# Output projections as seven block products a pair of tiles

## The reference

```python
    y = ... @ w_out                              # output projection, 2048 x 2048
    x = _layernorm(DEEPNORM_ALPHA * x + y, post_ln_g[i], post_ln_b[i])
    x = x + (p[i] @ ple_w[i]) * jax.nn.sigmoid(x @ ple_gate_w[i])
```

## Time and profile before

| | |
|---|---|
| median of 3 runs | 2100.16 us (2099.83 to 2100.18) |
| profiled execution, its own time | 2099.83 us |
| its span, first to last instruction | 2098.1 us |
| mean granted TensorE clock | 1.000 |
| DMA, mean over the span | 103 GB/s |

### The profile page before, as it was taken

The page is one execution under the profiler, slowest core; times in us unless marked ns, Lnnn a source line. Parts: engine busy times, 40 slices in busy tenths (PEclk is TensorE's granted clock), DMA queues, the critical chain, the costliest instruction groups (busy, mean ns, idle before and its releaser), DMA issues.

```text
span 2098.1 us, 28711 instructions
## 1 busy us (share of the span) xinstructions
PE 2091.8 (100%) x10510; PEld 1733.0 (83%) x10510; DVE 1256.2 (60%) x2105; ACT 817.0 (39%) x1042; POOL 362.0 (17%) x196
## 2 busy tenths in 40 slices
PE   9999999999999999999999999999999999999999
PEld 7878888888888888888788888888888888887888
DVE  5235575665665756356733588888888973567332
ACT  4225364464564656123622322222223441227221
POOL 0000000000000004000400034444757520004000
PEclk9999999999999999999999999999999999999999
DMA  8322222212222123322233322222222242222431
GB/s 319 141 102 93 70 77 80 80 62 79 81 80 80 60 80 137 133 84 97 99 113 123 135 100 86 96 101 100 100 87 93 100 181 100 92 92 77 142 111 68
DMA packets 33395, 216.76 MB, mean 103 GB/s; under 512 B 3952, under 2 KB 4224, under 8 KB 9520
## 3 DMA queue, kind: packets, MB, share of 16 engines
q1 hardware_dynamic: 28224, 189.54, 25.6%
q0 software_dynamic: 4816, 25.87, 3.1%
q10 hardware_dynamic: 288, 0.52, 0.1%
HBM read 207.53 MB, written 8.39 MB: 103 GB/s over the span
## 4 chain that ended last, share of the span: by engine, by line
PE 99%; ACT 1%; DMA 0%; DVE 0%; issue 0%; ACTq 0%
PE G L502 91%; PE X L502 5%; PE T L502 1%; PE T L685 1%; DMA Z<-xT_in 0%; PE T L806 0%; ACT a_hi L917 0%; ACT Z L1112 0%; ACT Y L1184 0%; PE T L811 0%; PE T L657 0%; ACT L1004 0%; DVE tmp L1451 0%; PE T L681 0%; DVE Y L1453 0%
## 5 line engine op out<-in xcount | busy, mean ns | idle before, releaser
L502 PE MATMUL G<-a_hi,w_hi 128*128 128x512 f32 x2764 | 1078.1, 390 | 0.6 <-ACT a_hi L917 0.6
L502 PE MATMUL G<-a_hi,w_lo 128*128 128x512 f32 x2764 | 1072.9, 388 | 0.0
L502 PE MATMUL G<-a_lo,w_hi 128*128 128x512 f32 x2764 | 1070.6, 388 | 0.0
L913 ACT ACTIVATE w_hi<-w_raw 128x2048 fp32r<-128x2048 f32 x173 | 331.5, 1916 | 946.2 <-PE G L502 933.3
L1312 DVE TENSOR_TENSOR w_lo<-w_raw,w_hi 128x2048 fp32r<-128x2048 f32 x128 | 297.1, 2321 | 640.3 <-ACT w_hi L913 640.3
L502 PEld LDWEIGHTS G<-a_hi,w_hi 128*128 128x128 f32 x2764 | 518.9, 188 | 110.3 <-ACT a_hi L917 1.5
L502 PEld LDWEIGHTS G<-a_hi,w_lo 128*128 128x128 f32 x2764 | 518.9, 188 | 107.2 <-issue 0.2
L502 PEld LDWEIGHTS G<-a_lo,w_hi 128*128 128x128 f32 x2764 | 519.0, 188 | 106.4 <-issue 0.5
L1895 DVE SCALAR_TENSOR_TENSOR T<-tmp,par,T 128x512 f32<-128x512 f32 x464 | 306.9, 751 | 0.0
L446 POOL TENSOR_TENSOR w_lo<-w_raw,w_hi 128x2048 fp32r<-128x2048 f32 x45 | 207.8, 4617 | 232.5 <-ACT w_hi L913 232.5
L410 POOL TENSOR_TENSOR a_lo<-Y,a_hi 128x512 fp32r<-128x512 f32 x32 | 44.2, 1397 | 366.9 <-ACT a_hi L917 366.6
(11 more groups left out here) (281 smaller groups left out, 1661.8 us busy)
## 6 DMA issues: line engine op xcount, KB each, us to landing
w_raw<-wall_in SPq DMA_DIRECT2D x174, 1024.0 KB, 4.8
Y<-xT_in POOLq DMA_DIRECT2D x5, 1024.0 KB, 7.2
Y<-w_in POOLq DMA_DIRECT2D x2, 2048.0 KB, 16.0
x_residual<-Y POOLq DMA_DIRECT2D x16, 256.0 KB, 3.8
Y<-x_residual POOLq DMA_DIRECT2D x4, 1024.0 KB, 5.3
out<-Y POOLq DMA_DIRECT2D x15, 256.0 KB, 3.7
w_raw<-wall_in SPq DMA_DIRECT2D x12, 256.0 KB, 7.9
Z<-xT_in SPq DMA_DIRECT2D x6, 512.0 KB, 9.0
```

The lines of the kernel that those rows point to most:

```text
L502: return pe.matmul(o, l, r, start=start, stop=stop)
L913: f(w_hi[:, w.slot, :], w_raw[:, w.slot, :], ACT.Copy).then_inc(S("w_hi"), 1)
```

## The change

Per layer, tiles 0 to 3 of the projection stay as they are. Tiles 4 to 13 become five pairs (p = 2 to 6), tiles 14 and 15 a sixth (p = 7). The two 2048-row tiles of a pair are cut into row blocks: r1 and r2 (the first 4 input chunks of either tile) and b11, b12, b21, b22 (the next 6 and the last 6 chunks). For p = 2 to 6 the b blocks, with the tokens cut into halves of 256, are multiplied as seven block products in place of eight: b11, t1, t3, t2, b22, b21, t4, each of 6 chunks by 256 tokens. The t pieces are sums of blocks, formed by GpSimd's DMAs that add into SBUF (`accum_op`); the operand sums ("folds", four of 6 chunks by 256 tokens) are formed once a layer by GpSimd and split by ScalarE and VectorE. VectorE puts the products together (`empty_first`, `empty_products`, `finish_one`, `finish_two`). Pair 7 is multiplied as before, in pieces.

Pieces pass through a ring of four slots in the space of `w_hi` and `w_lo`. The shift comes from four chunks, residual loads are moved (two of them to ScalarE's queue), the sums of the norm are spread over the pairs, many semaphores are merged, and p's load for layer 0 comes after the folds.

```diff
+PLAIN_K = 4
+PAIR_K = 6
+FOLDED = ("r1", "r2", "b11", "t1", "t3", "t2", "b22", "b21", "t4")
+FIRST_FOLDED = ("r1", "t1", "r2", "b11", "t3", "t2", "b22", "b21", "t4")
+UNFOLDED = ("r1", "r2", "b11", "b12", "b21", "b22")
...
 # GpSimd
+            def fold_operands(layer):
+                p = FOLD_FROM
+                pool.wait_ge(S("w_split"), W_OUT[layer] + 2 * p - 1)
+                load_first(layer, p, "t1", "b11")
+                for i in range(PAIR_K):
...
+                    if i >= 2:
+                        pool.wait_ge(S("fold_lo"), n - 1)
+                    raw = fold_raw[i % 2]
+                    pool.tensor_tensor(raw[:, 0:2, :], Y4[:, first, :, :], Y4[:, first:second + 1:PAIR_K, 1, :],
+                                       ALU.subtract).then_inc(S("fold_step"), 1)
+                    pool.wait_ge(S("fold_step"), 2 * n + 1)
+                    pool.tensor_tensor(raw[:, 2, :], raw[:, 1, :], Y4[:, first, 0, :], ALU.subtract).then_inc(S("fold_step"), 1)
+                    pool.wait_ge(S("fold_step"), 2 * n + 2)
+                    pool.tensor_tensor(raw[:, 3, :], raw[:, 2, :], Y4[:, second, 0, :], ALU.add).then_inc(S("fold_raw"), 1)
+                    if i == 1:
+                        add_second(layer, p, "t1", "b12")
+                        pool.wait_ge(S("w_split"), W_OUT[layer] + 2 * p)
+                        load_first(layer, p, "t3", "b12")
+                    if i == 3:
+                        add_second(layer, p, "t3", "b22")
+                    if i == 4:
+                        pool.wait_ge(*low_made(layer, p, "t1"))
+                        add_later(layer, p, "b22")
...
+            def add_later(layer, p, more):
+                pool.dma_start(source(p, "t2"), weights_of(layer, p, more), accum_op=ALU.add).then_inc(S("later_landed"), 16)
+            def weight_sums(layer):
+                for p in range(FOLD_FROM, FOLD_TO):
+                    if p > FOLD_FROM:
+                        add_second(layer, p, "t3", "b22")
+                        pool.wait_ge(*base_copied(layer, p))
+                        add_later(layer, p, "b22")
+                    if p + 1 < FOLD_TO:
...
+                        load_first(layer, p + 1, "t1", "b11")
+                        pool.wait_ge(*low_made(layer, p, "t3"))
+                        load_first(layer, p + 1, "t3", "b12")
+                    pool.wait_ge(*low_made(layer, p, "t2"))
+                    add_later(layer, p, "b21")
+                    if p + 1 < FOLD_TO:
+                        add_second(layer, p + 1, "t1", "b12")
...
 # TensorE
+            def piece_products(layer, p, name, out, highs, lows, start, stop):
+                pe.wait_ge(*low_made(layer, p, name))
...
+                for k in range(n):
+                    if (p, name) == (FOLD_FROM, "t1"):
+                        pe.wait_ge(S("fold_lo"), layer * PAIR_K + k + 1)
+                    at = slice(k * P, (k + 1) * P)
+                    mm(out, hi[:, at], highs[k], start and k == 0, False)
+                    mm(out, hi[:, at], lows[k], False, False)
+                    last = mm(out, lo[:, at], highs[k], False, stop and k == n - 1)
...
-                gemms(w + 2, g + 2, 6)
-                gemm(Idx(w + 8), Idx(g + 8))
-                shift(*after("half_summed", 2 * layer, KC // 2 + 2), (ones_r[:, :], sum_high[:, :]))
-                gemms(w + 9, g + 9, 6)
-                gemm(Idx(w + 15), Idx(g + 15))
+                gemm(Idx(w + 2), Idx(g + 2))
+                gemm(Idx(w + 3), Idx(g + 3))
+                for p in range(FOLD_FROM, FOLD_TO):
+                    folded_pair(layer, p)
+                pair_in_pieces(layer, FOLD_TO)
...
 # ScalarE, start of the stage
+                fold_high(0)
+                fold_high(1)
+                split(Idx(w + 3))
+                piece_high(p, "r1")
+                fold_high(2)
+                piece_high(p, "t1")
+                fold_high(3)
+                fold_high(4)
+                fold_high(5)
+                piece_high(p, "r2")
+                piece_high(p, "b11")
...
 # ScalarE, end of the stage
+                act.wait_ge(*landed(tile))
+                act.wait_ge(*piece_done(layer, FOLD_TO, "b21"))
+                f(w_hi[:, tile.slot, :], w_raw[:, tile.slot, :], ACT.Copy).then_inc(S("w_hi"), 1)
+                out_square(14)
                 load_root_table()
                 split(Idx(w + 17))
                 square(n_ln, KC - 1, ln_sq[1], KC - 2)
...
 # VectorE, start of the stage
+                half_sum(0)
+                split(Idx(w + 3))
+                half_sum(1)
+                fold_low(0)
+                fold_low(1)
+                half_sum(2)
+                p = FOLD_FROM
+                lows(p, "r1")
+                fold_low(2)
+                lows(p, "t1")
+                fold_low(3)
+                fold_low(4)
+                fold_low(5)
+                lows(p, "r2", "b11")
+                half_sum(3)
...
 # VectorE, a later pair
+                for p in range(FOLD_FROM + 1, FOLD_TO):
+                    c = SQUARES[p]
+                    lows(p, "r1")
+                    finish_two(p - 1)
+                    lows(p, "r2", "b11")
+                    finish_one(p - 1)
+                    full_add(2 * p - 2)
+                    lows(p, "t1")
+                    full_add(2 * p - 1)
+                    lows(p, "t3", "t2")
+                    empty_first(p)
+                    centres(CENTRES[p])
+                    if p > FOLD_FROM + 1:
+                        square_sums(c[:1])
+                    lows(p, "b22")
...
+                    lows(p, "b21")
+                    square_sums(c[-2:-1])
+                    lows(p, "t4")
+                    square_sums(c[-1:])
+                    empty_products(p)
...
 # VectorE, end of the stage
+                dve.wait_ge(*piece_done(layer, p, "b21"))
...
+                split(Idx(w + KC))
+                full_add(14)
+                centres(range(14, 15))
+                square_sums(range(14, 15))
                 out_chunk(Idx(w + 15), Idx(g + 15), KC - 1)
                 dve.wait_ge(*drained(Idx(g + 15)))
                 centre(n_ln, KC - 1)
```

More of the change, by code:

```diff
@@ L395, in _ @@
             pool.dma_start(w1_sb[0], w1[0]).then_inc(S("w1k_landed"), 16)
[L396 to L404, removed]
+            pool.dma_start(w1_sb[1], w1[1]).then_inc(S("w1v_w2_landed"), 16)
@@ new lines, in pair_in_pieces, with whole @@
+            def pair_in_pieces(layer, p):
+                g = G_OUT[layer] + 2 * p
+                one, two = out_banks(p)
+                pe.wait_ge(*drained(Idx(g - 4)))
+                pe.wait_ge(*drained(Idx(g - 3)))
+                def whole(lo, hi):
+                    return [a_hi[:, c, :] for c in range(lo, hi)], [a_lo[:, c, :] for c in range(lo, hi)]
+                middle = PLAIN_K + PAIR_K
+                done = S("piece_done")
+                piece_products(layer, p, "r1", one[:, :], *whole(0, PLAIN_K), True, False).then_inc(done, 1)
+                piece_products(layer, p, "r2", two[:, :], *whole(0, PLAIN_K), True, False).then_inc(done, 1)
+                piece_products(layer, p, "b11", one[:, :], *whole(PLAIN_K, middle), False, False).then_inc(done, 1)
+                piece_products(layer, p, "b12", two[:, :], *whole(PLAIN_K, middle), False, False).then_inc(done, 1)
+                piece_products(layer, p, "b21", one[:, :], *whole(middle, KC), False, True).then_inc(done, 1)
+                piece_products(layer, p, "b22", two[:, :], *whole(middle, KC), False, True).then_inc(
+                    S("gemm_done"), KC - 2 * FOLD_FROM)
@@ new lines, in second_part @@
+                piece_high(p, "b21")
+                piece_high(p, "t4")
+                for p in range(FOLD_FROM + 1, FOLD_TO):
+                    c = SQUARES[p]
+                    piece_high(p, "r1")
+                    piece_high(p, "r2")
+                    act.wait_ge(*summed(layer, p, "t1"))
+                    act.wait_ge(*low_made(layer, p - 1, "b21" if p == FOLD_FROM + 1 else "t4"))
+                    f(later, chain, ACT.Copy).then_inc(S("base_copied"), 1)
+                    piece_high(p, "b11")
+                    piece_high(p, "t1")
+                    if p == FOLD_FROM + 1:
+                        act.wait_ge(S("p_split"), 1)
+                        for n in range(2, 4):
+                            part = slice(4 * n * T, 4 * (n + 1) * T)
+                            act.dma_start(Y[:, part], (xT, x2_dram)[layer][:, part]).then_inc(S("res_landed2"), 16)
+                    piece_high(p, "t3")
+                    if p > FOLD_FROM + 1:
+                        out_square(c[0])
+                    piece_high(p, "t2")
+                    piece_high(p, "b22")
+                    piece_high(p, "b21")
+                    for n in c[-2:]:
+                        out_square(n)
+                    piece_high(p, "t4")
@@ new lines, in second_part @@
+                p = FOLD_TO
```

(13 more changed lines are left out.)

526 lines of the change are left out of this document (395 added, 131 removed).

## The result

The change makes the kernel slower: median 2128.21 us (2124.34 to 2128.66) against 2100.16, ratio 1.0129 with an interval of 1.0106 to 1.0152. The forecast was 2102, its range ended at 2113. The profiled execution is the one of 2124.34, its span 2122.6, which is 24.5 more than before.

What follows compares the result with a forecast made beforehand. TensorE, busy for the whole span, was taken as the bound. Gain -12.0, operand-sum waits +3.3 and +4.0, tail +6.4 and shared queues +0.8 made +2.5 us on 2099.83: 2102 us, range 2093 to 2113.

Steps and rivals of the forecast that it cites:

- The gain: Steady pairs of tiles on TensorE: 20.56 us instead of 21.76, so 12.0 us less for ten pairs in two layers.
- the tail: End of each layer: the PLE tile is split late, so token sums come late; 3.2 us lost a layer, 6.4 in all.
- Four later pairs at nothing: Pairs after the first folded one in each layer: VectorE has a margin of 2.1 us, so no cost.
- L: Time an adding DMA of weights takes to land: taken as 4.8 us, between 4.2 and 8.4, free up to 6.7.
- b21 for t4: The tight weight sum in a pair: 13.9 + L against 20.56 us, no cost up to L = 6.7.
- 0.8 us for contention: Second folded pair: ScalarE's two 1 MB residual DMAs share queues with the adds, 0.4 us taken a layer.
- Rival 2: Accumulating DMA slow: at L = 8.4 eight pairs wait 1.7 us each, first pairs 2.9; +19, 2121 us; 15%.
- The wait for operand sums: First folded pair: GpSimd's sums come late and TensorE waits 3.3 us in layer 0, 4.0 in layer 1.
- The bound: Operand-sum wait with GpSimd's twelve small instructions at 1.29 us each: 6.7 us more per layer.
- rival 3: GpSimd's 256-column instructions save little, or VectorE and GpSimd hold each other up: two waits grow by 3 each, 2108 us; 13%.
- Rival 4: Clock drops to 1.2 GHz after each of the two long waits: +4 to +7 us, 2107 us; 4%.
- The sum: All terms added: -12.0 + 3.3 + 4.0 + 6.4 + 0.8 = +2.5 us, giving 2102 us.

Runs made afterwards that it cites:

- e3: Changed kernel with the last pair's b21 and b22 in ring slots 2 and 3, tile 77 waiting for b12 and split ahead of chunk 14: 2120.02 us.
- e2: Changed kernel with the weight sums' adding DMAs writing instead, same bytes, order and waits: 2116.93 us.
- e4: Changed kernel with the residual's second quarter loaded behind the fourth operand sum and its last two as 512 KB in each of pairs 3 to 6: 2121.99 us.
- e9: Changed kernel with VectorE splitting operand sum 0, then second chunk sum, tile 64, sums 1 and 2; ScalarE and GpSimd orders changed to match: 2118.15 us.
- e5: Changed kernel with 14 extra 512-column matmuls, results unread, ahead of each of two operand-sum waits in the first folded pair: 2126.77 us.
- e1: Changed kernel with r2 and b11 taken ahead of t1 in the first folded pair of each layer: 2121.94 us.
- e12: e11 with the sixth operand sum formed by VectorE instead of GpSimd: 2096.37 us, ratio 0.9987 against the kernel before.
- e11: Changed kernel with e9's order, e3's ring slots, e4's residual loads, and VectorE splitting the next pair's r1 before emptying products: 2105.59 us.

## Why the prediction was wrong

**Right.** The gain (20.56 a pair; 20.58) and the tail (3.2 a layer; 3.0, mechanism and place shown by e3). Four later pairs at nothing: true of three; the second folded pair waits for its own weight sums.

**The step that failed first: the weight sums, L taken as 4.8 us, which "costs nothing up to L = 6.7".** I took one price, from loads that had the queues nearly to themselves. In the pairs where it counts L is 8 to 12. The chain also holds three adds in a row where I traced one (b21 for t4). The DMA share was never summed: a pair moves 200 GB/s at a share of 0.80 to 0.85 even in the steady state (before: 97 at 0.28), and the first two pairs have 3 MB of residuals and p's load besides. Where I had 0.8 us for contention, 10.1 were measured; e2 and e4 show that adding and load both have a part in it. Rival 2 named the mechanism (an add that takes 8 us); its price (+19) was for every pair, and it came with the sums of the first two only.

**The wait for operand sums: mechanism right, size half.** 6.5 + 6.7 for 3.3 + 4.0. The term that was mis-sized is GpSimd's sum: 256 columns at 0.73 us is right alone (0.74) and 1.07 to 1.62 beside VectorE; 512 columns take 1.29 alone, 2.14 at worst in this kernel. VectorE's split of a sum takes 1.23 alone and up to 2.13. The earlier trace rows showed such a stretch and I gave it 0.3 us. The Trainium skill (SBUF — State Buffer, Who interferes with whom) has the rule that I left out: a VectorE instruction with two SBUF inputs contends with a GpSimd instruction that reads SBUF, for a shared port that works as an exclusive lock. The rows agree in kind: alone 1.23 and 0.74, beside each other longer by 0.3 to 0.9. The bound was there (6.7 more a layer), and rival 3 (3 more in each wait) is what happened: 3.2 and 2.7 more.

**The clock.** Rival 4, at 4%, happened: 2.4 + 2.0 us behind the operand sums, 1.6 at a tail. The Trainium skill (TensorE: Matmul & The Clock Gate, Why this matters for your kernels) warns of gaps between bursts; the rows here agree in kind, 0.50 behind a wait, but not behind every one (1.00 behind 2.18 us, e9). e5 shows that the idle time lowered it there, since filling it kept 1.00. Even so the clock is not the whole of it: with the clock held, the time went to the weight sums.

**The sum.** I added waits as if each stood alone. e1 and e5 show that they overlap: taking 3.9 us or the slow matmuls away in layer 0 gave 1.8 us or all of it back at t4 and r1. Only e12, which takes four causes at once (operand sums, tail, residual loads, the queue ahead of r1), gets past the kernel before.

**Left open.** How much of the last 5.6 us in e12 is adding and how much load was not measured apart. The two other runs of the changed kernel, 4 us longer at a mean granted clock of 0.994 (0.996), have no trace. By these means some 8 us more of their spans were at the low level, an estimate, which is worth up to 4 us; e4's trace, also at 0.994, has such a stretch at the tail of layer 0 (0.50 from 1005 to 1011), where the changed kernel's has none. That it is the same in those two runs is argued.

## What to carry to other kernels

A cheaper product only pays in the steady state; price the entry and the exit of the loop by themselves, down to which instruction stands in front of which on each queue. Sum the bytes of a stage against what its DMA engines can move before giving a DMA a latency, and follow sums that depend on sums as one chain. When TensorE has been busy throughout, count the slow matmuls that may follow each new wait as part of its price: here up to 2.5 us behind one wait, and nothing behind another of much the same length.

## What the runs showed of the hardware

- The length of a wait alone does not tell whether the clock falls. Behind 2.51 us of idle time it fell (e1, 0.50), and behind 1.72 (e12, 0.71 over the 5 us around it); behind 2.18 (e9, layer 0) and 1.91 (915.66 of the changed kernel, 1.00 from 916 to 936) it did not. The same three waits at the tail left it at 1.00 in layer 0 of the changed kernel and at 0.66 in layer 1.
- A VectorE subtraction of 2048 columns beside a run of GpSimd subtractions ends in one of two ways. In twelve of the traces it takes 3.4 us and GpSimd's fifteen 21.3; in the traces of e3 and e11 it takes 9.6, and GpSimd 18.7. TensorE then waits 6.3 us for it. One GpSimd instruction takes 1.3 us, and 9.6 less the 2.29 that VectorE's takes alone is more than five of them; if the port is what it waits for, it stands back that often in a row, which is argued. Rows of e3:

```profile
807.63 18.69 POOL L682 TENSOR_TENSOR a_lo<-Y,a_hi 128x512 fp32r<-128x512 f32 x15 [339.56 <-DVE Z L1922]
```

```profile
818.90 9.58 DVE L1710 TENSOR_TENSOR w_lo<-w_raw,w_hi 128x2048 fp32r<-128x2048 f32 x1 [2.19 <-ACT w_hi L1246]
```

  Beside e9 to e11, the kernel before ran 13 times at 2099.3 to 2100.6 us and 10 times at 2106.6 to 2108.2, which fits the same event; no trace shows it in that kernel.
- An adding DMA of 384 KB uses 64 more packets than a plain one and some 1.1 us of all 16 engines (8.0% of 2122.6 us less 5.9% of 2116.5, over 40 adds).
